# Mean matmuls of the RMS norms in pairs on the two column halves of the array, the halves added by VectorE, in a decoder trunk on 8 cores

## What is computed

```python
def rmsnorm(x, g):
    xf = x.astype(jnp.float32)
    y = xf * lax.rsqrt(jnp.mean(xf * xf, axis=-1, keepdims=True) + RMS_EPS)
    return (y * g.astype(jnp.float32)).astype(x.dtype)

def decoder_layer(x, ...):
    x = x + 0.5 * swiglu(rmsnorm(x, norm_ffn1), ...)    # gate/up, down (1024 -> 2816 -> 1024)
    h = rmsnorm(x, norm_mix)
    z = h @ w_in                                        # pool input, q, k, v, two gates
    ...                                                 # causal pooling, dilated window attention
    merged = gates[:, :, 0] * pool_br + gates[:, :, 1] * attn_br
    x = x + merged @ w_o
    x = x + 0.5 * swiglu(rmsnorm(x, norm_ffn2), ...)
    return x                                            # then a final rmsnorm
```

## Time and profile before

| | us |
|---|---|
| median of 3 runs | 2925.41 |
| lowest | 2922.5 |
| the profiled execution | 2923.13 |
| its span, slowest core (4) | 2921.9 |
| spans of the other cores | 2911.1 to 2921.3 |

### The profile page before, as it was taken

How to read it: one execution, slowest core, us unless ns; L and a number is a source line. 1 busy time by engine, 2 the same in 40 slices (tenths; PEclk the granted TensorE clock), 3 DMA queues, 4 the chain that set the end, 5 groups by cost and what they waited for, 6 DMA issues and landing times.

```text
span 2921.9 us, 47174 instructions; the slowest of 8 cores (2911.1 to 2921.9 us)
## 1 busy us (share of the span) xinstructions
PE 2815.1 (96%) x16993; PEld 1350.6 (46%) x17306; DVE 1038.7 (36%) x1704; ACT 755.7 (26%) x1340; POOL 331.0 (11%) x448
## 2 busy tenths in 40 slices
PE   7999988999999999999999999999999999999997
PEld 2444544444444455444444445444444445544443
DVE  3212753421241166442142128542124216644112
ACT  2111233312121124421122113432112112442111
POOL 1000620000000044000000007000000004400000
PEclk8999998999999999999999999999999999999999
DMA  9666765765353334343343424344224223433221
GB/s 212 146 150 134 192 150 139 182 171 139 107 173 107 110 125 153 109 146 127 103 152 110 138 80 149 125 131 148 83 75 165 71 89 119 144 118 114 73 75 70
DMA packets 97089, 372.58 MB, mean 128 GB/s; under 512 B 12472, under 2 KB 14168, under 8 KB 93660
## 3 DMA queue, kind: packets, MB, share of 16 engines
q1 hardware_dynamic: 75760, 270.81, 27.7%
q0 software_dynamic: 17648, 86.94, 13.9%
q10 hardware_dynamic: 3456, 11.80, 1.0%
HBM read 342.66 MB, written 99.03 MB: 151 GB/s over the span
## 4 chain that ended last, share of the span: by engine, by line
PE 89%; DVE 4%; issue 3%; DMA 2%; ACT 1%; ACTq 0%; SPq 0%; DVEq 0%; POOL 0%; POOLq 0%
PE ps L198 89%; DMA sb_xT<-x 1%; DVE sb_hT L507 1%; DMA sb_uexs<-spoolT 1%; DVE sb_ystg L507 1%; DMA kp<-sb_kf 1%; DVE sb_rtmp L579 1%; DVE sb_pbuf L765 0%; DVE sb_V L214 0%; DVE sb_kf L579 0%; DVE sb_kf L917 0%; ACT sb_pbuf L761 0%; ACT sb_V L213 0%; DMA sb_kT<-kcs 0%; DVE sb_mergedT L919 0%
## 5 line engine op out<-in xcount | busy, mean ns | idle before, releaser
L198 PE MATMUL ps<-sb_hT,sb_w 128*128 128x512 bf16 x7461 | 1685.2, 381 | 31.6 <-issue 6.3
L198 PEld LDWEIGHTS ps<-sb_hT,sb_w 128*128 128x128 bf16 x7680 | 740.6, 98 | 920.2 <-issue 61.0
L525 ACT ACTIVATE sb_stmp<-ps 128x512 f32<-128x512 f32 x352 | 209.8, 597 | 920.5 <-PE ps L198 871.2
L198 PE MATMUL ps<-sb_actTB,sb_w 128*128 128x512 bf16 x1371 | 316.6, 379 | 1.8
L198 PE MATMUL ps<-sb_actTA,sb_w 128*128 128x512 bf16 x1382 | 316.2, 379 | 1.8 <-DVE sb_actTs L526 0.2
L468 ACT ACTIVATE sb_sq<-sb_xT 128x512 bf16<-128x512 f32 x224 | 139.4, 630 | 666.7 <-DVE sb_xT L570 467.3
L526 DVE TENSOR_TENSOR sb_actTB<-sb_stmp,ps 128x512 bf16<-128x512 f32 x176 | 120.9, 687 | 485.8 <-PE ps L198 472.3
L526 DVE TENSOR_TENSOR sb_actTA<-sb_stmp,ps 128x512 bf16<-128x512 f32 x176 | 119.9, 686 | 421.1 <-PE ps L198 417.1
L570 DVE SCALAR_TENSOR_TENSOR sb_xT<-ps,sb_xT 128x512 f32<-128x512 f32 x128 | 87.8, 690 | 434.3 <-PE ps L198 421.2
L198 PEld LDWEIGHTS ps<-sb_actTA,sb_w 128*128 128x128 bf16 x1408 | 136.9, 98 | 163.7 <-issue 0.2
L198 PEld LDWEIGHTS ps<-sb_actTB,sb_w 128*128 128x128 bf16 x1408 | 136.7, 98 | 163.7
(11 more groups left out here) (134 smaller groups left out, 1528.5 us busy)
## 6 DMA issues: line engine op xcount, KB each, us to landing
sb_w<-wscr SPq DMA_DIRECT2D x341, 512.0 KB, 4.0
sb_w<-wch POOLq DMA_DIRECT2D x83, 512.0 KB, 8.3
wscr<-sb_w SPq DMA_DIRECT2D x83, 512.0 KB, 4.5
sb_w<-wscr SPq DMA_DIRECT2D x52, 384.0 KB, 3.5
kvs<-c POOLq DMA_DIRECT2D x32, 511.8 KB, 5.0
y<-sb_ystg POOLq DMA_DIRECT2D x7, 2048.0 KB, 12.1
sb_xT<-x SPq DMA_DIRECT2D x8, 1024.0 KB, 11.9
sb_xT<-x SPq DMA_DIRECT2D x4, 2048.0 KB, 10.8
```

Source lines behind the costliest of these rows:

```text
L198: self.pe.op(lambda: self.nc.tensor.matmul(out, lhsT, rhs, start=start, stop=stop, **kw), reads=reads, writes=writes, inc=inc)
L525: act.op(lambda: nc.scalar.activation(out=st[:, 0:n], in_=ps[bg][:, 0:n], func=AF.Silu), reads=[psr[bg]], writes=st.r)
```

## The change

`flush` now takes the pending squares two at a time. The first square of a pair is multiplied by the left 64 columns of `meanm` into rows 0 to 63 of the bank, the second by the same 64 columns into rows 64 to 127. Each half accumulates four matmuls. The first of a pair waits for both squares, and only the second signals. A single pending square stays until a second has joined it, so its buffer must not be handed out again: `sq_live` keeps the buffers that wait. Since each half of the bank now holds half of the mean, `head` copies the upper half to the lower partitions of rstd (ScalarE), adds the lower half of the bank (VectorE), makes Ln on 64 partitions, and Exp twice, to the upper and to the lower 64 partitions.

```diff
             def add(self, c, eng=None):
                 seg, n = self.seg, self.seg.n
                 ring_ = sqb if n == T else sqs
+                assert any(id(x) not in sq_live for x in ring_)
+                while id(ring_[sq_i[0] % len(ring_)]) in sq_live:
+                    sq_i[0] += 1
                 sq = ring_[sq_i[0] % len(ring_)]
                 sq_i[0] += 1
+                sq_live.add(id(sq))
...
             def flush(self):
-                for sq in self.pend:
-                    i = self.n_mm
-                    self.n_mm += 1
-                    K.mm(ps[self.b][:, 0:self.seg.n], meanm[:], sq[:, 0:self.seg.n], i == 0, i == 7, reads=sq.r + meanm.r,
-                         writes=[psr[self.b]], inc=True)
-                self.pend = []
+
+                while len(self.pend) > 1:
+                    pair, self.pend = self.pend[:2], self.pend[2:]
+                    for k, sq in enumerate(pair):
+                        i = self.n_mm
+                        self.n_mm += 1
+                        K.mm(ps[self.b][64 * k:64 * k + 64, 0:self.seg.n], meanm[:, 0:64], sq[:, 0:self.seg.n], i < 2, i > 5,
+                             reads=pair[0].r + pair[1].r + meanm.r if k == 0 else (), writes=[psr[self.b]] if k == 0 else (), inc=(k == 1))
+                        sq_live.discard(id(sq))
+                    EngW.commit((pe.sem, pe.cnt), pair[0].r + pair[1].r, [psr[self.b]])
...
             def head(self):
                 assert self.n_mm == 8 and not self.pend
                 seg, n, b = self.seg, self.seg.n, self.b
-                act.op(lambda: nc.scalar.activation(out=seg.rstd[:, 0:n], in_=ps[b][:, 0:n], func=AF.Ln, bias=EPS, scale=1.0),
-                       reads=[psr[b]], writes=seg.rstd.r)
-                act.op(lambda: nc.scalar.activation(out=seg.rstd[:, 0:n], in_=seg.rstd[:, 0:n], func=AF.Exp, scale=-0.5), reads=seg.rstd.r,
+                lo, hi = slice(0, 64), slice(64, 128)
+                act.op(lambda: nc.scalar.copy(out=seg.rstd[lo, 0:n], in_=ps[b][hi, 0:n]), reads=[psr[b]], writes=seg.rstd.r)
+                dve.op(lambda: nc.vector.tensor_tensor(out=seg.rstd[lo, 0:n], in0=seg.rstd[lo, 0:n], in1=ps[b][lo, 0:n], op=ALU.add),
+                       reads=[psr[b]] + seg.rstd.r, writes=seg.rstd.r)
+                act.op(lambda: nc.scalar.activation(out=seg.rstd[lo, 0:n], in_=seg.rstd[lo, 0:n], func=AF.Ln, bias=EPS, scale=1.0),
+                       reads=seg.rstd.r, writes=seg.rstd.r)
+                act.op(lambda: nc.scalar.activation(out=seg.rstd[hi, 0:n], in_=seg.rstd[lo, 0:n], func=AF.Exp, scale=-0.5), reads=seg.rstd.r,
+                       writes=seg.rstd.r)
+                act.op(lambda: nc.scalar.activation(out=seg.rstd[lo, 0:n], in_=seg.rstd[lo, 0:n], func=AF.Exp, scale=-0.5), reads=seg.rstd.r,
                        writes=seg.rstd.r)
                 K.give(b)
```

More of the change, by code:

```diff
@@ L452, in build @@
         sq_i = [0]
+        sq_live = set()
         class Norm:
```

## The result

The changed kernel takes 2993.24 us (median; 2990.93 to 3047.71) where the kernel before took 2924.73 in the same comparison: ratio 1.0234, 95% interval 1.0211 to 1.0257. It is slower by 68 us. The prediction was 2951 us, range 2928 to 2978: the direction was right, the size was not, and "within 2%" was wrong. In some executions the cores of one die run at a lower clock whatever the kernel; the ratios leave those out, and where a median would mix them in I give the lowest time, or the mean span over the dies that ran at their usual clock.

The account below looks back on a forecast made before the run. TensorE, with 89% of the chain, was taken to bound the kernel. 2923.1 us plus 29.7 for the heads, less 5.8 for the pairs, plus 4 for the clock gave 2951 us, range 2928 to 2978.

Parts of the forecast that it names:

- What bounds the kernel: Whole kernel: TensorE holds 89% of the chain; time changes only by its stream's length or by its standing still.
- The pairs: Mean matmuls in TensorE's stream: a lone pair gains 0.02 us, two adjacent pairs 0.23; 5.8 us less in sum.
- Rivals 1: Switching to column halves costs nothing, as the 64-column weights are loaded ahead: 21 us less, 2930 us; chance 9%.
- 3 (no overlap): The two halves of a pair don't overlap, a pair costs 0.43 + 0.19: 26 us more, 2977 us; chance 8%.
- Rival 4: Clock falls in the norm pairs, each a small break in TensorE's stream: over 2% slower, 3055 us; chance 3%.
- The head: Each norm, last mean matmul to first scaling: 2.0 us longer, 1.25 where ScalarE loads a table for Ln.
- Where the head shows: Places where the longer head lies on TensorE's path: 29.7 us in sum, all other heads hidden.
- the projections and attention: B's norm before the projections: head hidden by a whole projection of the other tile on TensorE, 0 us.
- the gates: Gates of the second tile, four times: table load before Ln, nothing left to hide the head, 1.25 each, 5.0 us.
- B's first norm: First norm of the second tile, pairs 1 to 3: head 1.75 us later, 0.8 each showing, 2.4 us.
- the sample block: Second gate/up stage of pair 0: ScalarE blocked behind VectorE's add for the sample uses up 8 PSUM banks, 0.5 us.
- The clock: Behind three grown stalls the granted clock may fall, 0 to 2.8 us each, 8.4 in all; taken as 4 us.

Follow-up runs that it names:

- the undone order: Changed kernel with the heads of all segments issued before the first scaling of any: 2982.75 us, ratio 1.0188.
- the run with three copies: Kernel before with three ScalarE copies of rstd onto itself between Ln and Exp in each head: 2980.67 us, ratio 1.0195.
- the shorter head: Changed kernel with four head steps in a row instead of five, both halves copied across, one add, Ln and Exp on 128 partitions: 2977.09 us lowest, ratio 1.0212.

## Why the prediction was wrong

**What bounds the kernel** was right: TensorE sets the end, and time moved only by what made it stand or by its own rate.

**The pairs.** Entering 0.31, both halves together, double pairs: right within 0.02. The way out is 0.34, so a lone pair gains nothing; the sum is -1 to -3, not -5.8. At the measured prices my count of 102 lone pairs and 9 doubles gives +1.1 and -1.9. Rivals 1 (no price for the switch) and 3 (no overlap) fall with the same rows, and the halves overlap, but a lone pair spends the whole saving on its two switches. The Trainium skill ("TensorE: Matmul & The Clock Gate", Part 3) states that matmuls on different column tiles overlap and start some 4 ns apart; by that alone 26 us would have come, an estimate. The trace agrees with the overlap (the two of a pair start 0.004 us apart, 52.1 us busy for 88.6) and not with that sum. Rival 4 (the clock falls in the pairs): the 200 us from 600 to 800, second gate/up and down projection of pair 0 with their pairs, stand within 1 us of before, without half clock. What I gave as its sign, a mean clock under 0.97, didn't come (0.977), though the clock was the second largest part of the miss, behind stalls and not in pairs.

**The head** was 2.21, not 2.0. With 29.7 as the sum, that is 10% of it, 3 us.

**Where the head shows** is the step that failed. I priced nine terms and took the other heads as hidden "by at least two gate/up units or a whole projection of the other tile". Measured: 26 to 31 us for each us of head on ScalarE alone (20 without the clock), and 35 with VectorE's part (77 for 2.21), where my 29.7 for 2.0 is 15 for each. The misses are of three kinds. Places held as hidden that were not: the projections and attention, 23 us in the table and 15 in the mean of the cores, 5 of it the clock. At the entry of pair 0's attention that is VectorE's backlog, which a late head shifts, with the banks it frees; the other stretches I did not take apart beyond the waits given above. Places priced too low, the gates (11.3 for 5.0) and B's first norm (6.2 for 2.4): I had "the add runs beneath the load", 1.25 us for such a head and 1.75 behind a product. The load starts after the add, so they are 2.2 and 3.1. For the gates that is 4 x 2.2 = 8.8 for my 5.0, and 2.9 of clock come on top; for B's first norm 3 x 1.36 = 4.1 more than my 2.4, 6.5 in all. And the queue that is blocked across engines: the sample block, 6.7 for 0.5, by a wrong count of free banks (the undone order gave 6.7 back).

**The clock** was one term of 4 us, with 8.4 as its most. It is 25. The price of a fall was inside the 0 to 2.8 that I allowed (1.5 to 1.7 us in the comparisons above); their number was not: I counted three grown stalls, while the granted clock of core 0 is at its half level in 8 stretches before and in 22 after. The clock's term has to be taken per stall, with the stall's new length, as it multiplies each error in the sum before it.

**VectorE's part** had only the add's 0.69 in the chain. The add's place in VectorE's queue costs up to 20 us of the head's 77, which only the run with three copies showed. Half of it is the sample's add behind B's scalings: with that order undone 9.3 us came back. How the rest divides between VectorE standing at the add and its added 0.69 us is not shown; the occupancy alone is excluded by the shorter head.

**The range** came from a third of the heads' sum either way. A list of places that I called hidden, each costed at nothing, should have been in it: I wrote that without cover each would cost 2.0 and then left that out of the bounds.

## What to carry to other kernels

A step between two engines that recurs at every norm is best priced by its length times the number of all its occurrences, and only then reduced by covers that the trace shows to be idle: here 20 us for each us over 32 norms, so some two thirds were exposed, and 27 with the clock that fell behind the longer waits. A cover must be looked for on the engine that is delayed, not only for the result that is late. Before a step is put beneath a table load, look whether the load itself waits for that step: here it did, 12 times of 12. Idle matmuls keep the clock up only where they start inside the wait: a filler that needs a bank which isn't free comes on top of the stall.

## What the runs showed of the hardware beyond that

Two column halves of one bank run fully together, but going in and out costs 0.09 and 0.12 us, so a lone pair of 512-column matmuls is worth nothing (0.443 against 0.432 us) and each further pair in a row saves 0.22. A table load for ScalarE's Ln started only after the add that Ln waits for (863.87 behind an add that ended at 863.79). Behind stalls of nearly the same length (2.34 and 2.44 us) the clock once fell and once didn't (granted clock 0.72 and 1.00). A step on 64 partitions lasts as long as on 128 (ScalarE's Exp 0.64 both ways; VectorE's add with a PSUM operand 0.68 in the changed kernel and 0.69 on 128 partitions in the one with the shorter head, in the mean of 32).
